# Splitting the modulated features on VectorE alone, with two unrounded tiles from ScalarE, and the first two weight groups split a stage earlier

## The reference

```
for l in range(2):
    sh1, sc1, g1, sh2, sc2, g2 = split(silu(c) @ w_mod[l] + b_mod[l], 6)
    u  = x   * (1 + sc1)  + sh1            # the "modulated" features, 512 tokens
    uc = ctx * (1 + csc1) + csh1           # the same for 256 context tokens
    y, yc = token_mixer(u, uc, ...)        # u @ w_in: conv, cq, ckv, gates, o, qkv parts,
                                           # attention, mLSTM, convolution; then three
                                           # branches, each gated with sigmoid(u @ w_gates)
    x = layer_norm(alpha * x + g1 * y)
    x = layer_norm(alpha * x + g2 * mlp(x * (1 + sc2) + sh2))
```

## Time and profile before

| | us |
|---|---|
| runs | 3590.85, 3592.05, 3592.59 (median 3592.05) |
| the profiled execution | 3593.69 |
| its span, first to last instruction | 3591.9 |
| TensorE busy in the span | 3341.1 (93%) |
| VectorE, ScalarE, GpSimd busy | 1849.3, 1160.8, 1148.2 |

### The profile page before, as it was taken

The page is one execution under the profiler, slowest core; times in us unless marked ns, Lnnn a source line. Parts: engine busy times, 40 slices in busy tenths (PEclk is TensorE's granted clock), DMA queues, the critical chain, the costliest instruction groups (busy, mean ns, idle before and its releaser), DMA issues. The chain is left out here.

```text
span 3591.9 us, 50713 instructions
## 1 busy us (share of the span) xinstructions
PE 3341.1 (93%) x19112; PEld 2702.1 (75%) x19112; DVE 1849.3 (51%) x2677; ACT 1160.8 (32%) x1744; POOL 1148.2 (32%) x567
## 2 busy tenths in 40 slices
PE   4999999899999999996899988998999979799998
PEld 3888566688878888884677666886899757588785
DVE  3769444612348243244786545127433466777525
ACT  1223333512234222123232434224323364322223
POOL 3423001422223322232431013443444333344442
PEclk7999999899999999997999997999999989899998
DMA  5222254022221222221222330332333321233232
GB/s 170 63 56 57 46 153 136 1 54 66 62 59 55 64 65 60 65 65 36 75 71 51 106 112 13 94 94 77 90 93 94 88 64 53 60 99 93 83 94 75
DMA packets 549132, 270.16 MB, mean 75 GB/s; under 512 B 55922, under 2 KB 547146, under 8 KB 548827
## 3 DMA queue, kind: packets, MB, share of 16 engines
q1 hardware_dynamic: 547330, 267.20, 26.4%
q10 hardware_dynamic: 889, 0.30, 0.0%
q0 software_dynamic: 736, 0.17, 0.0%
HBM read 265.50 MB, written 2.10 MB: 75 GB/s over the span
## 5 line engine op out<-in xcount | busy, mean ns | idle before, releaser
L374 POOL TENSOR_TENSOR weights_low<-weight_ring,weights_high 128x1024 fp32r<-128x1024 f32 (+1 forms) x408 | 985.0, 2416 | 1703.0 <-ACT weights_high L365 1662.3
L365 ACT ACTIVATE weights_high<-weight_ring 128x1024 fp32r<-128x1024 f32 (+1 forms) x408 | 409.6, 1006 | 1387.0 <-PE ps L459 1319.0
L454 PE MATMUL ps<-u_high,weights_high 128*128 128x512 f32 (+1 forms) x1440 | 536.4, 382 | 59.6 <-DVE u_low L772 43.0
L455 PE MATMUL ps<-u_low,weights_high 128*128 128x512 f32 (+1 forms) x1440 | 524.0, 374 | 0.0
L454 PEld LDWEIGHTS ps<-u_high,weights_high 128*128 128x128 f32 x1440 | 277.4, 193 | 126.8 <-issue 37.4
L454 PE MATMUL ps<-hidden_high,weights_high 128*128 128x512 f32 x960 | 334.7, 361 | 16.7 <-DVE hidden_low L2365 16.7
L455 PE MATMUL ps<-hidden_low,weights_high 128*128 128x512 f32 x960 | 332.3, 361 | 0.0
L459 PE MATMUL ps<-u_high,weights_low 128*128 128x512 f32 (+1 forms) x1440 | 316.1, 367 | 1.9 <-POOL weights_low L374 1.9
L455 PEld LDWEIGHTS ps<-u_low,weights_high 128*128 128x128 f32 x1440 | 277.6, 193 | 52.0 <-issue 3.7
L1122 DVE SCALAR_TENSOR_TENSOR conv<-conv,vectors 128x512 f32<-128x512 f32 x360 | 293.2, 866 | 31.8 <-DVE conv L1122 28.8
L454 PE MATMUL ps<-mlp_u_high,weights_high 128*128 128x512 f32 (+3 forms) x1024 | 287.7, 311 | 10.8 <-DVE mlp_u_low L2416 7.2
(11 more groups left out here) (515 smaller groups left out, 5452.3 us busy)
## 6 DMA issues: line engine op xcount, KB each, us to landing
weight_ring<-in_w_in SPq DMA_DIRECT2D x262, 256.0 KB, 3.2
weight_ring<-in_w SPq DMA_DIRECT2D x256, 256.0 KB, 3.1
weight_ring<-in_w_mod SPq DMA_DIRECT2D x192, 256.0 KB, 3.8
weight_ring<-in_w_up SPq DMA_DIRECT2D x88, 256.0 KB, 3.1
weight_ring<-in_w_out SPq DMA_DIRECT2D x48, 256.0 KB, 3.2
weight_ring<-in_w_down SPq DMA_DIRECT2D x32, 256.0 KB, 3.2
weight_ring<-in_w_mla_out SPq DMA_DIRECT2D x32, 128.0 KB, 2.3
weight_ring<-in_w_conv_out SPq DMA_DIRECT2D x32, 128.0 KB, 2.3
```

The lines of the kernel that those rows point to most:

```text
L365: act.activation(core.ring_high[:, split_slot(run, q), 0:n], core.ring[:, slot, 0:n], ACT.Copy).then_inc(core.high_ready.sem, 1)
L374: core.nc.gpsimd.tensor_tensor(core.ring_low[:, split_slot(run, q), 0:n], core.ring[:, (run.first + q) % SLOTS, 0:n], high.bitcast(F32), A ...
L454: pe.matmul(to, w_high[:, k, 0:m], high(k, a, b), start=(first and k == 0), stop=False, skip_group_check=True)
L455: pe.matmul(to, w_high[:, k, 0:m], low(k, a, b), start=False, stop=False, skip_group_check=True)
```

## The change

In the four places where `Modulated` works, GpSimd has no feature tile any more: VectorE makes all eight low parts. ScalarE makes the unrounded tiles 3 and 6 (`ACT_TILES`) behind its high parts of the same tiles, with a new semaphore for them, so that VectorE modulates six tiles in place of eight.

The low parts of the first two weight groups are made by GpSimd at the end of the stage ahead (`first_low_parts`): in setup for layer 0's projection, at the end of both mLSTM stages for the merge, and in the norm stage for layer 1's projection. For layer 0's projection the high parts move to setup as well. GpSimd's two clearings in the projection stage move behind the convolution's eight weight groups. No arithmetic is changed.

```diff
-def low_parts(core, pool, *runs):
+def low_parts(core, pool, *runs, made=0):
...
+        for q in order[ahead_of:] if unrolled else []:
+            low_part(core, pool, run, 0, q)
+        whole = n if n >= 3 else unrolled
+        if whole > unrolled:
+            with pool.Fori(unrolled, whole) as i:
...
+def first_low_parts(core, pool, run):
+
+    order = [x for x in range(run.body) if run.split[x]]
+    for q in order[:LEAD]:
+        low_part(core, pool, run, 0, q)
...
             load_vectors(pool, 0, SHARE, pool_loaded)
+            first_low_parts(core, pool, core.runs["conv0"])
...
             act.activation(mod_rows[:, half:], in_rows[:, half:], ACT.Copy).then_inc(rows_copied.sem, 1)
+            first_high_parts(core, act, core.runs["conv0"])
...
+ACT_TILES = (3, 6)
...
             ins.then_inc(self.high_made.sem, 1)
...
+            if k in ACT_TILES:
+                self.wait(act, k - 2)
+                for j, a, b in self.spans:
+                    ins = act.activation(self.tmp[:, k % 2, a:b], self.core.x[:, k, a:b], ACT.Identity, scale=self.scale(k, j),
+                                         bias=self.shift(k, j))
+                ins.then_inc(self.made_by_act.sem, 1)
...
         for k in range(KT + 1):
-            if k < KT:
+            if k < KT and k not in ACT_TILES:
                 if k >= 2:
...
-            if k and k - 1 not in POOL_TILES:
-                self.low_part(dve, k - 1, self.ready)
-
-    def make_low_besides(self, pool):
-
-        for k in POOL_TILES:
-            self.low_part(pool, k, self.pool_ready)
+            if k:
+                self.low_part(dve, k - 1)
+
+    def low_part(self, dve, k):
+
+        by_act = sum(x < k for x in ACT_TILES)
+        if k in ACT_TILES:
+            dve.wait_ge(self.made_by_act.sem, self.made_by_act.at(by_act + 1))
+        else:
+            dve.wait_ge(self.made.sem, self.made.at(k + 1 - by_act))
+        dve.wait_ge(self.high_made.sem, self.high_made.at(k + 1))
...
@@ project_stage, GpSimd
-            core.u.make_low_besides(pool)
+            low_parts(core, pool, runs["conv"], made=LEAD)
             nc.gpsimd.memset(rows[gates.both], 0.0).then_inc(cleared.sem, 1)
             nc.gpsimd.memset(core.gates[gates.both, 0:T + 32], 0.0).then_inc(cleared.sem, 1)
-            low_parts(core, pool, *list(runs.values())[:-1])
+            low_parts(core, pool, *list(runs.values())[1:-1])
...
@@ project_stage, ScalarE
-            if both:
-
-                first_high_parts(core, act, runs["conv"])
             core.u.make_high(act)
...
@@ norm_stage, GpSimd
+            if following and following != "in2":
+                first_low_parts(core, pool, core.runs[following])
...
@@ mlstm_stage, GpSimd
+            first_low_parts(core, pool, core.runs[f"{BRANCHES[0][0]} branch{l}"])
...
@@ merge_stage, GpSimd
-            core.u.make_low_besides(pool)
-            low_parts(core, pool, *runs)
+            low_parts(core, pool, *runs, made=LEAD)
```

More of the change, by code:

```diff
@@ L375, in low_part @@
                                  high.bitcast(F32), ALU.subtract).then_inc(core.split_ready.sem, 1)
-def low_parts(core, pool, *runs):
-    for run in runs:
+def low_parts(core, pool, *runs, made=0):
+    for r, run in enumerate(runs):
         n = run.groups // run.body
-        whole = n if n >= 3 else 0
-        if whole:
-            with pool.Fori(0, whole) as i:
+        ahead_of = made if r == 0 else 0
+        order = [x for x in range(run.body) if run.split[x]]
+        unrolled = 1 if ahead_of else 0
+        for q in order[ahead_of:] if unrolled else []:
[3 more added lines that the diff above has]
+            with pool.Fori(unrolled, whole) as i:
                 for q in range(run.body):
@@ L786, in make_low @@
                 ins.then_inc(self.made.sem, 1)
-            if k and k - 1 not in POOL_TILES:
-                self.low_part(dve, k - 1, self.ready)
-    def make_low_besides(self, pool):
-        for k in POOL_TILES:
-            self.low_part(pool, k, self.pool_ready)
+            if k:
[7 more added lines that the diff above has]
+        dve.wait_ge(self.high_made.sem, self.high_made.at(k + 1))
+        dve.tensor_tensor(self.low[:, k, 0:self.w], self.tmp[:, k % 2, 0:self.w], self.high[:, k, 0:self.w].bitcast(F32),
+                          ALU.subtract).then_inc(self.ready.sem, 1)
     def passed(self):
-        super().passed(KT, len(POOL_TILES))
+        self.made.passed(KT - len(ACT_TILES))
+        self.made_by_act.passed(len(ACT_TILES))
+        self.high_made.passed(KT)
+        self.ready.passed(KT)
 def spread_sums(core, pe, out, tiles, first, last):
```

10 lines of the change are left out of this document (1 added, 9 removed).

## The result

| | before | after |
|---|---|---|
| median of the runs, us | 3592.32 (4 runs, 3590.85 to 3592.87) | 3561.95 (4 runs, 3559.22 to 3564.68) |
| profiled execution, its span, us | 3593.69, 3591.9 | 3560.26, 3558.4 |
| mean granted TensorE clock | 0.954 | 0.962 |

The ratio is 0.991, 95% interval 0.9898 to 0.9922: 30 us less by the medians, 33.5 us by the two profiled spans. The forecast was 3570.6, with a range of 3561 to 3579: the direction is right, and the median lies 1 us inside the lower edge. By the ratio, applied to the 3592.05 that the forecast started from, the time is 3559.7, 1.3 us outside it, and two later comparisons of the same kernel gave 3560.37 and 3558.83 against 3593.47 and 3594.52, also outside. The sum said 21.4 us: 9 us more were gained by the medians, 12.1 by the profiles.

What follows compares the result with a forecast made beforehand. TensorE was taken as the bound, with time to win at stage starts. The sum 32.3 - 6.1 - 4.8 = 21.4 us, against the median of 3592.05, gave 3570.6 us, range 3561 to 3579.

Steps and rivals of the forecast that it cites:

- the reading of the 10.31 us: Layer 0's projection start: four modulating instructions take 10.31 us, not 1.70, because VectorE stands still while GpSimd tensor instructions run.
- The pieces: VectorE's work at the four stage starts gets shorter by 11.2, 6.3, 9.6 and 5.2 us, together 32.3.
- The walk: Stage starts, VectorE's new order low part by low part: the last ends 13.1 us after its start for wide tiles.
- ScalarE's two tiles: Stage starts: ScalarE making 10 tiles in place of 8 costs only a 0.2 us wait at the end.
- The mLSTM stage ends: Both mLSTM stages: the barrier waits for GpSimd's two subtractions, so the merges start later; cost 2.9 + 3.2 = 6.1 us.
- The norm stage: Ahead of layer 1's projection: two GpSimd subtractions hold VectorE's chain on SBUF operands, both taken in full; cost 4.8 us.
- the rival price of 3.4: Norm stage: were VectorE always first, both subtractions would wait for its whole chain; cost 3.4 us.
- The clearings at 0: GpSimd's two memsets, moved beside convolution taps, cost nothing; up to 3.8 us per layer in VectorE's chain if they held taps.
- Not in the sum is TensorE's clock: Stage starts: with no 8 us pause the clock might stay up, 0 to 6 us more or the other way; unsummed.
- TensorE has its groups as before: Behind each stage start nothing else comes due earlier, so the gains should add up to the end.
- The backlog: Stage starts: the last two low parts come 1.1 us apart, not 0.9; maybe 0.5 us a stage, left out.
- the second: Rival, chance 0.22: clock stays up in two or three stages (4 us), norm stage pays 3.4, not 4.8; 3565.

Runs made afterwards that it cites:

- e1: Changed kernel with only the feature part kept: weight groups' low parts, clearings and layer 0's roundings back where they stood before; 3572.66 us, ratio 0.9949.
- e2: Changed kernel with only the weights part kept: GpSimd has feature tiles 1, 3 and 5 again, two weight groups still split a stage ahead; 3572.29 us, ratio 0.9947.
- e5: Changed kernel with GpSimd's two clearings ahead of the projection's later weight groups again, in both layers; 3567.24 us, ratio 0.9932.
- e4: Changed kernel, but ScalarE makes no unrounded tile and VectorE modulates all eight; 3572.63 us, ratio 0.994.
- e6: Changed kernel with layer 1's first two weight groups rounded at the norm stage's start, so GpSimd subtracts before VectorE's chain; 3561.56 us, ratio 0.9917.
- e11: The changed kernel profiled a third time, with no edit; 3558.83 us, ratio 0.99.
- e9: Changed kernel with only the first weight group subtracted a stage ahead, and in the norm stage at the stage's start; 3553.07 us, ratio 0.9883.
- e8: Changed kernel with 131 added unused matmuls, 115 behind TensorE's last norm-stage work and 16 ahead of layer 1's projection; 3567.83 us, ratio 0.9934.

## Why the prediction was right in its main mechanism and too small in its size

- *VectorE stands still while GpSimd works* (the reading of the 10.31 us): right. e1 and e2 take away one half of GpSimd's work each and the pieces follow; e5 adds it back for the clearings. No modulating instruction is over 0.60 us after.
- *The pieces*: 32.3 us forecast, 33.0 measured. The walk gave 13.1 us for three of them; they are 13.11, 13.03 and 13.12. The fourth was given as 8.7 and is 8.15.
- *ScalarE's two tiles*: they cost 0.6 us of waits at the end of a piece, not 0.2, and are worth 4.3 us over the four (e4). That the piece is 13.1 us all the same is luck in a small thing: VectorE's own work in it takes 12.5 us, not 12.9.
- *The mLSTM stage ends*, 2.9 and 3.2 us: right in the mechanism. The wait at the barrier went from 0.42 to 3.08 us and from 0.42 to 3.48, 2.7 and 3.1 us. Against e1, which has no subtractions there, the sections are 2.8 and 3.0 us longer. In layer 1 the clock hid part of it: the section grew by 1.75 only, and the same 376 matmuls took 1.3 us less of TensorE's time.
- *The norm stage*, 4.8 us with both subtractions in full on the path: 4.04, shown by e6. The step "I take both in full" was a fifth too large, and the rival price of 3.4 (VectorE always first) too small. They alternate, each subtraction costs VectorE 2.02 us, and itself takes 0.75 longer. Of what the prediction quotes from the Trainium skill, page "SBUF — State Buffer", section "Who interferes with whom", the lock for a whole instruction is borne out by these rows, and who issues first changes from one instruction to the next.
- *The clearings at 0*: right for where they went; the stretch behind layer 0's first group is 282.76 us with them, as before. The prediction listed them among what fills the 10.31 us without a share of their own; e5 gives it, 5.5 us of the pieces' 33.0.
- *What failed* is the paragraph "Not in the sum is TensorE's clock", which put two terms at nothing, and the sentence that behind each stage start "TensorE has its groups as before". The paragraph named the right place: behind the last low part 4.5 us were gained. The backlog that it left out, "0.5 us a stage", was 1.8 us in four stages, close to what it said. The clock, "0 to 6 us more" or as much the other way, was valued at nothing in the middle, and gave 2.7: three of four tails ran at 1.00, where they had run at 0.59 to 0.73. Its reason, that the pause of 8 us goes, is not enough: it is gone in e2 too, and the tails there are as long as before. And the clock reached further than the starts: in six stretches whose work is the same the profile has another 4.2 us less (6.7 in e11's), which no line of the sum had. The groups were as before and their time wasn't: TensorE was busy 3107.9 us on them after and 3112.8 before. Together 8.7 of the 12.1 us by which the profiles miss the sum; the rest is 1.4 in the mLSTM sections, 0.7 or 0.8 each in the norm stage, the pieces and setup.
- Of the rivals, the second (the clock stays up in two or three starts, 3565) came nearest; with the norm stage at 4.0 and the 4.2 us of the unchanged work it gives some 3561. Its 4 us in the starts are 4.5, though in part by the backlog.

The last part of this isn't a property of the change that could be planned. In thirteen profiles the six stretches took 3239.5 to 3250.5 us: 3246.3 before (twice), 3242.1, 3242.2 and 3239.5 after, 3240.2 and 3239.9 in the halves, 3250.5, 3250.3, 3247.8, 3245.0, 3248.5 and 3245.4 in e4 to e9. The changed kernel stands at the good end, twice the same. What decides where the bits fall stays open: they differ between variants and mostly repeat with a program, and no run shows the rule.

## What to carry to other kernels

Count GpSimd's instructions beside every VectorE stretch that sets a stage's start: clearings count too where VectorE modulates from one SBUF operand. Moving them a stage ahead costs nothing where that stage has a gap in VectorE's SBUF work and slack at its barrier (setup, e6); without these it still paid here, 24.4 us in the pieces for 8.8. One group ahead and early in the stage was 6 us better than two groups at its end. A forecast of a few us on a kernel that TensorE bounds needs a line for the granted clock: give the work behind each removed pause at both levels, and add some 5 us either way for stretches that nobody touched. Judge an edit by its own section in the profile, since e6 moved its section by 4.04 us and the time by nothing. Where TensorE works in the section, even that isn't enough: layer 0's mLSTM section has the same work in the changed kernel and in e8 and takes 93.81 and 89.23 us, at 0.86 and 0.90 of full clock; VectorE's wait at the barrier is steadier there (3.08 and 3.06 us).

## What the runs showed of the hardware

- A GpSimd subtraction of 2.3 us (alone) in the midst of VectorE instructions on two SBUF operands delays them by 2.02 us, and is itself stretched to 3.1; four one-operand instructions beside one of 1.82 us are delayed by 1.53.
- The granted clock was at a mean of 0.72 over 6 us in which TensorE was busy without a pause, at the start of an attention stage (layer 0 in the changed kernel, behind a pause of 1.43 us), and at 1.00 in another execution of the same kernel. Each such fall costs 1.65 us.
- Keeping TensorE busy with matmuls of no use held the clock at 0.98 for 25.8 us; some 6 us behind the last of all added matmuls it fell again, in the piece where TensorE works and pauses in turns.
